# Feed-forward up products of ten groups as seven 2x2 block products instead of eight

## What is computed

```python
D_FF = ((8 * D_MODEL // 3 + 127) // 128) * 128        # 2816

def conv_gated_mlp(n, w_up, conv_w, conv_b, w_down):
    u = n @ w_up                                       # 1024 x 1024 by 1024 x 5632
    c = u.shape[-1]
    u = lax.conv_general_dilated(
        u, conv_w.astype(u.dtype)[:, None, :], window_strides=(1,),
        padding=[(CONV_WIDTH - 1, 0)], dimension_numbers=('NWC', 'WIO', 'NWC'),
        feature_group_count=c) + conv_b.astype(u.dtype)
    gate, val = u[..., :D_FF], u[..., D_FF:]
    return (jax.nn.silu(gate) * val) @ w_down
...
        n = rms_norm(h, ln_ffn_g[l])
        h = h + conv_gated_mlp(n, w_up[l], conv_w[l], conv_b[l], w_down[l])
```

## Time and profile before

| | us |
|---|---|
| median of three runs (2962.46 to 2968.52) | 2968.47 |
| the profiled execution | 2962.56 |
| its span, first to last instruction | 2960.8 |
| PE busy, of the span | 2847.0 (96%) |
| POOL busy, of the span | 804.0 (27%) |
| mean granted clock of TensorE | 0.986 |

### The profile page before, as it was taken

One profiled execution on the slowest core, in us unless ns is written; L12 is line 12 of the kernel. 1 busy time (PEld: TensorE's weight loads), 2 busy tenths in 40 slices (PEclk: granted clock), 3 DMA queues, 4 the chain that ended last, 5 costly groups with the idle time before them and its releaser, 6 DMA issues.

```text
span 2960.8 us, 36189 instructions
## 1 busy us (share of the span) xinstructions
PE 2847.0 (96%) x13519; PEld 2250.4 (76%) x13536; DVE 1498.7 (51%) x1790; ACT 943.9 (32%) x1536; POOL 804.0 (27%) x498
## 2 busy tenths in 40 slices
PE   6999999999999999999999999999999999999998
PEld 5888886676777777778888888887787777777776
DVE  6464556654534436364434433334336665477764
ACT  4322226755400004231221111212214444254441
POOL 5312203433333331122332332321221101321225
PEclk8999999999999998999999999999999999999999
DMA  6200100000211110001111111111210001000023
GB/s 206 79 22 24 42 8 15 22 22 20 76 48 46 46 48 22 29 29 50 50 43 50 47 45 50 43 49 36 86 37 23 17 21 26 11 6 6 16 105 116
DMA packets 166337, 128.57 MB, mean 43 GB/s; under 512 B 19264, under 2 KB 150048, under 8 KB 165968
## 3 DMA queue, kind: packets, MB, share of 16 engines
q1 hardware_dynamic: 164816, 118.55, 13.2%
q10 hardware_dynamic: 1408, 8.50, 0.7%
HBM read 114.20 MB, written 12.65 MB: 43 GB/s over the span
## 4 chain that ended last, share of the span: by engine, by line
PE 86%; DVE 7%; ACT 3%; issue 2%; DMA 1%; POOL 1%; SPq 0%; ACTq 0%; DVEq 0%; POOLq 0%
PE ps L753 21%; PE ps L754 21%; PE ps L755 21%; PE ps L2856 2%; PE ps L2696 2%; PE ps L2572 2%; PE ps L2563 2%; PE ps L665 1%; PE ps L2494 1%; PE ps L2464 1%; PE ps L2751 1%; PE ps L2952 1%; PE ps L2752 1%; PE ps L2753 1%; PE ps L2953 1%
## 5 line engine op out<-in xcount | busy, mean ns | idle before, releaser
L753 PE MATMUL ps<-NH,w_high 128*128 128x512 f32 (+2 forms) x1992 | 772.9, 388 | 14.2 <-POOL w_low L1111 8.0
L754 PE MATMUL ps<-NL,w_high 128*128 128x512 f32 (+2 forms) x1992 | 773.3, 388 | 0.0
L755 PE MATMUL ps<-NH,w_low 128*128 128x512 f32 (+2 forms) x1992 | 770.1, 387 | 0.0
L1109 POOL CAST w_high<-w_raw 128x1024 fp32r<-128x1024 f32 x193 | 208.4, 1080 | 1932.2 <-PE ps L755 1159.3
L1111 POOL TENSOR_TENSOR w_low<-w_raw,w_high 128x1024 fp32r<-128x1024 f32 x193 | 482.0, 2497 | 15.4
L753 PEld LDWEIGHTS ps<-NH,w_high 128*128 128x128 f32 x1992 | 376.9, 189 | 99.9 <-issue 9.0
L754 PEld LDWEIGHTS ps<-NL,w_high 128*128 128x128 f32 x1992 | 376.2, 189 | 78.3 <-issue 0.9
L755 PEld LDWEIGHTS ps<-NH,w_low 128*128 128x128 f32 x1992 | 377.0, 189 | 76.9
L858 DVE TENSOR_TENSOR hT<-hT,ps 128x1024 f32<-128x1024 f32 x168 | 205.0, 1221 | 227.5 <-PE ps L755 227.5
L753 PE MATMUL ps<-act_high,w_high 128*128 128x512 f32 x352 | 141.4, 402 | 2.9 <-DVE act_low L1999 2.9
L755 PE MATMUL ps<-act_high,w_low 128*128 128x512 f32 x352 | 139.4, 396 | 0.0
(11 more groups left out here) (411 smaller groups left out, 5291.9 us busy)
## 6 DMA issues: line engine op xcount, KB each, us to landing
w_raw<-in_w_in SPq DMA_DIRECT2D x69, 512.0 KB, 3.8
w_raw<-in_w_up SPq DMA_DIRECT2D x44, 512.0 KB, 3.8
w_raw<-in_w_out SPq DMA_DIRECT2D x24, 512.0 KB, 3.4
w_raw<-in_w_down SPq DMA_DIRECT2D x22, 512.0 KB, 3.7
w_raw<-in_w_xkv SPq DMA_DIRECT2D x8, 512.0 KB, 5.8
x_in<-in_x SPq DMA_DIRECT2D x8, 512.0 KB, 9.0
residual_spill<-hT SPq DMA_DIRECT2D x1, 4096.0 KB, 13.6
hT<-residual_spill ACTq DMA_DIRECT2D x1, 4096.0 KB, 13.0
```

Of the source, the lines that this page charges most:

```text
L753: nc.tensor.matmul(o, wh, xh, start=start, stop=False)
L754: nc.tensor.matmul(o, wh, xl, start=False, stop=False)
L755: return nc.tensor.matmul(o, wl, xh, start=False, stop=stop)
L1109: nc.gpsimd.tensor_copy(WH[slot][:, :], w_raw[slot][:, :]).then_inc(w_high, 1)
```

## The change

For groups 1 to 10, one tile of gate columns and the value tile that belongs to it are taken as a 2x2 block matrix, gate and value on one side and the two halves of the 1024-long sum on the other, and the normed activations as 2x2 blocks too, the halves of the sum by the halves of the tokens. The product of the two is made with seven block products in Strassen's manner (Winograd's form) in place of eight. A block product is 4 chunks by 3 passes, 12 matmuls. With weights A11, A12 (first and second half of the sum for the gate), A21, A22 (for the value):

- POOL makes the sums of weight blocks in `w_raw`, S3 = A11 - A21, S1 = A21 + A22, S2 = A22 - S3, S4 = A12 - S2, and splits each of A11, A12, S1, S2, S4, S3, A22 into high and low parts of 128x512. The old `WH` and `WL` are now a ring of four half tiles.
- DVE makes the four sums of activation blocks once (`block_sums`, 128x2048 each), ACT their high parts, DVE their low parts.
- PE runs the seven products in four banks (SUM, TWO_SUM, OTHER, LAST). Three of the outputs are running sums: ACT copies a bank out between two products that add into it (`copied`), and DVE adds banks onto these copies (`added`).
- SP loads only what a ring slot's raw buffer allows: the two tiles of a pair, then the two tiles of the down weights, then the next pair.
- The ten rounds are written out. Round n has the pair (n,0), the down products of group n-1, and the pair (n,1). There are two buffers for copied-out up products (`uu`) where there were four, two for convolutions (`cc`) where there were four, and the parts of the gated product lie in the unused end of `NH` and `NL`.

Group 0 and stage F1 keep their products; what goes before and after stays as it was. The core of the diff:

```diff
+            def step(ins):
+                steps[0] += 1
+                ins.then_inc(b_step, 1)
+                pool.wait_ge(b_step, steps[0])
+            def split_block(raw, to, count):
+                high, low = to
+                step(nc.gpsimd.tensor_copy(high, raw))
+                nc.gpsimd.tensor_tensor(low, raw, high.bitcast(F32), ALU.subtract).then_inc(b_ready, 1)
+                pool.wait_ge(b_ready, count)
+            def blocks(n, x):
+                done, ready = 7 * group(n, x) + 7, of_tile(n, x)
...
+                pool.wait_ge(b_raw[0], count)
...
+                elif x == 0:
+                    pool.wait_ge(b_prod, done - 2)
+                else:
+                    wait_done(pool, FFN, n - 1, 3)
+                split_block(r11, ring[RING_A11], ready + 1)
+                pool.wait_ge(b_raw[1], count)
+                step(nc.gpsimd.tensor_tensor(r11, r11, r21, ALU.subtract))
+                step(nc.gpsimd.tensor_tensor(r21, r21, r22, ALU.add))
...
+                split_block(r12, ring[RING_A12], ready + 2)
...
+                else:
+                    wait_done(pool, FFN, n - 1, 7)
+                split_block(r21, ring[RING_S1], ready + 3)
+                step(nc.gpsimd.tensor_tensor(r21, r22, r11, ALU.subtract))
+                split_block(r21, ring[RING_S2], ready + 4)
+                step(nc.gpsimd.tensor_tensor(r12, r12, r21, ALU.subtract))
+                pool.wait_ge(b_prod, done + 1)
+                split_block(r12, ring[RING_S4], ready + 5)
+                pool.wait_ge(b_prod, done + 2)
+                split_block(r11, ring[RING_S3], ready + 6)
+                pool.wait_ge(b_prod, done + 3)
+                split_block(r22, ring[RING_A22], ready + 7)
...
+            for n in FN:
+                blocks(n, 0)
+                for x in range(2):
+                    down_split(n, x)
+                blocks(n, 1)
...
+            def up_blocks(n, x):
+                for v in range(2):
...
+                    elif x == 0:
+                        sp.wait_ge(b_ready, of_tile(n - 1, 1) + 6 + v)
+                    else:
+                        sp.wait_ge(b_ready, of_down(n, v))
...
+            def down_blocks(n):
+                for x in range(2):
+                    sp.wait_ge(b_ready, of_tile(n, 0) + 6 + x)
...
-            with pe.Fori(0, FFN.iters) as i:
-                dense(pe, FFN, i, 0, 0, NH, NL)
-                pe.wait_ge(f_lo, i * 2 + 4)
-                update(pe, FFN, i, 1, 1, aH, aL, 2)
-                for k in range(1, 4):
-                    dense(pe, FFN, i, 8 + k, 2 + k, NH, NL)
+                    product(n, x, 1, RING_A11, first_half(0), SUM, True, False)
+                    product(n, x, 2, RING_A12, first_half(4), OTHER, True, True)
...
+                    product(n, x, 3, RING_S1, block_sums(0), TWO_SUM, True, False)
...
+                    pe.wait_ge(b_snap, 4 * g + 4 + 1)
+                    product(n, x, 4, RING_S2, block_sums(1), SUM, False, False)
+                    pe.wait_ge(b_snap, 4 * g + 4 + 2)
+                    product(n, x, 5, RING_S4, later_half(4), TWO_SUM, False, True)
...
+                    product(n, x, 6, RING_S3, block_sums(2), SUM, False, True)
...
+                    product(n, x, 7, RING_A22, block_sums(3), LAST, True, True)
+                    if x == 0:
+                        pe.wait_ge(f_lo, 2 * n + 2)
+                        for f in range(C):
+                            if f % 4 == 0:
+                                pe.wait_ge(b_ready, of_down(n, f // 4))
```

More of the change, by code:

```diff
@@ L1152, in one @@
                 split(n % 2, n)
-            assert third % 2 == 1
-            tiles(ahead + 12, third - 1)
+            assert third % 2 == 1 and F1.w0 % 2 == 0
+            tiles(ahead + 12, F1.w0)
+            steps = [0]
+            def step(ins):
[7 more added lines that the diff above has]
+                pool.wait_ge(b_ready, count)
@@ L1156, in _ @@
+            for n in FN:
+                blocks(n, 0)
+                for x in range(2):
+                    down_split(n, x)
+                blocks(n, 1)
+            for x in range(2):
+                pool.wait_ge(b_prod, 7 * group(FN[-1], 1) + 13 + x)
+                one(F1.w0 + x)
+            tiles(F1.w0 + 2, third - 1)
             one(third - 1)
@@ new lines, in silu, with high @@
+            def silu(n, x):
+                act.wait_ge(f_tap, n * 4 + (2 * x + 1))
+                nc.scalar.activation(cc[0][:, :], cc[0][:, :], ACT.Silu).then_inc(f_act, 1)
+            def high(n, x):
+                act.wait_ge(f_prod, n * 2 + (x + 1))
+                if n == 0:
+                    act.wait_ge(tile_done, F0.tile(0, 4))
+                elif x == 0:
+                    wait_done(act, FFN, n - 1, 7)
+                nc.scalar.activation(aH[x], cc[1][:, :].rearrange("p (a b) -> p a b", a=2), ACT.Copy).then_inc(f_hi, 1)
@@ L2015, in _ @@
+            taps(FN[-1], 1, 1)
+            product(FN[-1], 1)
+            low(FN[-1], 1)
             add_update(dve, F1, 0, 0)
@@ new lines, in _, with product @@
+            block_sums = lambda n: (lambda c: (TH[:, n, c, :], TL[:, n, c, :]))
+            def product(n, x, at, slot, operand, o, start, stop):
+                pe.wait_ge(b_ready, of_tile(n, x) + at)
+                high, low = ring[slot]
+                for c in range(4):
+                    cs = slice(c * P, (c + 1) * P)
+                    xh, xl = operand(c)
+                    nc.tensor.matmul(o, high[:, cs], xh, start=(start and c == 0), stop=False, skip_group_check=True)
+                    nc.tensor.matmul(o, high[:, cs], xl, start=False, stop=False, skip_group_check=True)
+                    mm = nc.tensor.matmul(o, low[:, cs], xh, start=False, stop=(stop and c == 3), skip_group_check=True)
+                mm.then_inc(b_prod, 1)
```

327 lines of the change are left out of this document (231 added, 96 removed).

## The result

The changed kernel takes 3024.76 us (median of 4 runs, 3023.99 to 3029.20), the kernel before 2967.70 on the same chip (4 runs). The ratio is 1.0201, with a 95% interval of 1.0188 to 1.0213: 2% slower, as forecast (3020, range 2966 to 3062). The profiled execution has a span of 3022.0, 61.2 longer than before.

What follows compares the result with a forecast made beforehand. POOL's chain of splits, sums and loads was taken to bound the changed kernel: 63.6 + 7.4 = 71.0 a round against 66.9. With rounds 41, start 6, end 2, clock 8: 2962.6 + 57-us terms listed = 3019.6, 3020 us; range 2966 to 3062.

Steps and rivals of the forecast that it cites:

- The cycle: One FFN-loop round along POOL's chain of splits, loads and down products: 63.6 us, 71.0 with collisions, against 66.9 before.
- the splits: Cycle step on POOL after the last down product: splits of S1, S2, S4, S3 and two sums, 10.86 us.
- the two loads: Raw-buffer reloads behind S3, for the next pair and for the down weights: 4.03 us each, A22's split inside.
- The collisions: DVE instructions with both inputs in SBUF delay POOL in the loop: eight on its chain at 0.92, 7.4 us a round.
- The clock: PE's clock falls after its wait for down weights, 1.7 us each, in half of ten rounds: 8 us, between 0 and 17.
- the last step: End of the cycle: PE's start, 96 down products (22.38 us) and POOL's release (0.30), together 22.98 plus clock.
- the start: Before the loop, DVE's block sums slow POOL's split of F0's third tile: 4 later, 2 for clock; 6 us, between 2 and 10.
- the end: Behind product 7, gate taps, an addition and silu stand ahead of the value's chain: 2 us more, between 0 and 4.
- Whole-length collisions: Rival: each loop collision costs a whole tap, 1.28, and the clock falls every round; 73.8 a round, 3057 us. Chance 0.13.
- the second rival: DVE's taps fall into POOL's waits in the loop: round 63.6 to 64.9, time 2938 to 2951 us. Chance 0.11.
- collisions hardly reach the chain: Claim that DVE's taps fall into POOL's waits: below 0.4 us for each of eight instructions; 2938 to 2951 us. Chance 0.11.
- PE stays the bound: Rival: only the removed matmuls count in the loop, 55.6 us less plus 8 for the ends: 2915 us. Chance 0.03.

Runs made afterwards that it cites:

- filler: Changed kernel plus thirteen extra matmuls on ready operands just before PE waits for a round's first down weights: 3011.03 us, ratio 1.0150.
- no_taps: Changed kernel with the convolution's value taps on DVE writing 32 columns in place of 510 to 512: 2959.66 us, ratio 0.9972.
- start: Changed kernel with DVE's four block sums of the first feed-forward half put behind the first taps: 3029.01 us, ratio 1.0211.
- after: The changed kernel itself, with the seven block products, against the kernel before: 3024.76 us, ratio 1.0201.
- thin: Changed kernel with POOL's low parts of the ring's blocks cut to 32 of 512 columns: 2922.18 us, ratio 0.9863.
- halves: Changed kernel with raw weights loaded as four half tiles, each load waiting only for its half to fall free: 2994.71 us, ratio 1.0099.
- order: halves with DVE's first residual addition of the down products ahead of the value tap, the second ahead of the next tap: 2968.86 us, ratio 1.0006.
- casts3: order with ACT, not POOL, casting twelve of eighteen high parts a round plus the first pair's S1, S2, S4, and some steps reordered: 2936.69 us.

## Why the prediction was right, and where its terms were off

**The cycle.** It forecast a round of 71.0 without the clock; the mean is 72.53, and 70.80 where filler gives back 1.73 of the clock. The agreement is not only one of the total: in the mean of eight rounds the splits take 10.86 for 10.86, the two loads 4.03 and 3.98 for 4.03. The cast that no row showed was taken at 0.61 and is 0.61. PE's waits are of the kind that was named, the longest (3.9) ahead of the down products, though shorter in total: some 7 a round where 9 were forecast.

**The collisions.** Nine instructions of DVE were forecast to collide, eight on the chain at 0.92, 7.4; the rounds have these nine, and the eight cost 6.92. The ninth is what the prediction read wrongly: it was let "fall into a wait for a load", and it does, but the next load is issued behind it, so it came back as the late second buffer, 0.9 a round, where the prediction has that buffer arrive "just as A11 has been split". So the eight cost 0.5 a round less than forecast, and the ninth 0.9 more. Additions of a bank cost nothing, as read from the earlier trace rows: 0.68 beside POOL.

The rule weighed was that of the Trainium skill, SBUF — State Buffer, section Who interferes with whom: the pair of ports that DVE and GpSimd share is an exclusive lock, it says, and a DVE instruction with two SBUF inputs contends with a GpSimd instruction that reads SBUF. The section's words that the pair is held for the whole instruction stand beside DVE's two-port modes; that they hold for the taps too was the prediction's reading. The rows agree in kind, since on half tiles a cast of 0.61 and a subtraction of 1.29 lose nearly the same, 0.83 to 0.88, which has nothing to do with their own length; in size they do not reach the 1.28 of a whole tap, nor does the whole tile at 1662.95, which lost 1.05.

**The clock.** This is the step that was mis-sized most. A fall was priced at 1.7, and the nine that PE's rows show cost 1.9 in the mean. The count was wrong: "I let half of the ten fall", 8 us in all, where nine of ten fell, 17 us. Without a fall the last step takes 22.61 in no_taps, 0.4 less than the 22.98 of the forecast. In each of eight windows of 72 us from 1368 to 1944 the granted clock is below 1.00 (0.93 to 0.98), and filler gave back 13.7.

**Start and end.** 6 was forecast for the start, 4 for a later job and 2 for the clock. PE waited 5.64 for the third job's weights where it waited 2.26 before, and the 13 matmuls behind that wait took 5.57 in place of 13 x 0.2331 = 3.03: 3.4 and 2.5, 5.9 together. That the wait can't simply be moved away is what start shows. For the end 2 was forecast: from the last up matmul (2007.68 before, 2070.73 now) to the first small matmul of the next norm (2027.97 and 2093.00) it is 20.3 before and 22.3 now, 2.0 more.

**The sum.** 49 for the rounds with the clock, 6 and 2; measured 10 x (72.53 - 66.88) = 56.5, 5.9 and 2.0. These make 64.4, and the traces have 64.7 between the last matmul ahead of the third job (1314.09 and 1314.43) and that small matmul. The spans differ by less, 61.2, since from there to the end the kernel after takes 929.0 and the one before 932.8. The change does not touch that stretch, and in the other ten kernels' profiled executions it takes 929.2 to 933.6. So it is in part luck that the forecast of 3020 is only 5 us off: the rounds cost 7.5 more than forecast (the terms above, each read by itself, make 9: some 9 each for the clock and the ninth collision, less 5 for the other eight and 4 for the last step), and 3.8 came back outside them.

**The rivals.** Whole-length collisions fell with the 0.83 to 0.88 on the chain; the clock of that rival, falling in every round, came nearly true. That collisions hardly reach the chain fell with no_taps. That PE stays the bound (2915) is what thin shows at 2922, with most of POOL's low parts cut away. The remark in the second rival, that the value tap ahead of the first addition would hold the third down product, came true as soon as the loads were out of the way: 1.97 a round in halves.

halves gains 30 in time and 41 in ten rounds. Most of the difference, 7.5, is no price of its edit. In its profiled execution the first silu of the stage comes 2.5 later than in after (1326.03 and 1323.51), and from the last one to the end of the span it takes 5.0 longer (952.16 and 947.20), both in work that the edit does not touch. order, which has the same loads, shows neither (1322.92 and 947.44).

What stays open is why the clock did not fall behind the one wait of 2.72 and fell behind waits of 2.59 and 2.79; no run was made for it.

## What to carry to other kernels

A cut in the busiest engine's work is worth only what the chain that feeds it allows: before moving work to an engine that is 27% busy, walk one round of its instructions in order, with buffers, loads and the other engines' instructions that it collides with, and compare that walk with the round. A collision that falls into a wait for a load is not free when the next load is issued behind it. When the walk is too long, mend in the order in which the waits appear, since each mended wait shows the next (loads, a tap ahead of an addition, casts). Taking work off the feeding engine helped here only where it was taken from the stretch that the bound engine waits for: twelve casts moved gave nothing, three more in the right place, with the order around them, gave 34 us.

## What the runs showed of the hardware that was not expected

- A collision of POOL with a DVE tap costs POOL's half tiles nearly a constant: 0.88 for the cast of 0.61 and 0.83 to 0.88 for the subtraction of 1.29 (1.49 and 2.12 to 2.16; in eight rounds a single one lost more, 1.05). The whole-tile subtraction, 2.40 alone, took 3.45 beside a tap that had begun 0.06 ahead of it (1662.89): 1.05.
- ACT's casts of 128x512 do not take part. In casts3 some of them ran beside the same taps; all 145 in one line (duration ns min/median/max, first and last start):

```profile
L1608 ACT ACTIVATE w_high<-w_raw x145: 610/624/637, 1353.7 to 1973.3; 128x512 fp32r<-128x512 f32 x145
```

- Waits of PE of 2.59 to 3.94 ahead of the down products were followed by a stretch at half clock in nine of ten rounds, of 5.3 us behind the wait of 3.46; 2.75 us of extra matmuls in its place, which compute nothing, kept the clock at 1.00 there, and a round became 1.73 shorter.
